# A hybrid attention and retention layer on one core: output jobs behind the next unit's query jobs, halves added in PSUM, a third job bank, x loaded transposed

## What is computed

```python
h = rms_norm(x, norm_gain)
proj = jnp.einsum('bsd,de->bse', h, w_in)
aq, ak, av, ag, rq, rk, rv, rg = jnp.split(proj, SPLIT_POINTS, axis=-1)
attn = window_attention(aq, ak, av, q_norm_gain, k_norm_gain, sink_logits)  # 16 heads, 4 kv heads, 64 wide, 2 chunks of 64
ret = retention(rq, rk, rv, ret_norm_gain)          # 8 heads, state carried over the chunks, group norm per head
mixed = jnp.concatenate([attn * jax.nn.silu(ag), ret * jax.nn.silu(rg)], axis=-1)
x = x + jnp.einsum('bse,ed->bsd', mixed, w_out)
```

## Time and profile before

| | |
|---|---|
| median of 3 runs | 1658.97 us (1658.12 to 1659.2) |
| the profiled execution's own time | 1657.89 us |
| its span, first to last instruction | 1656.1 us |
| busy PE / PEld | 96% / 83% |
| busy DVE / ACT / POOL | 70% / 41% / 27% |
| DMA | 320.49 MB, mean 194 GB/s |
| mean granted PE clock | 0.996 of 2.4 GHz |

### The profile page before, as it was taken

How to read it: one execution, slowest core, us unless ns; L and a number is a source line. 1 busy time by engine, 2 the same in 40 slices (tenths; PEclk the granted TensorE clock), 3 DMA queues, 4 the chain that set the end, 5 groups by cost and what they waited for, 6 DMA issues and landing times.

```text
span 1656.1 us, 24605 instructions
## 1 busy us (share of the span) xinstructions
PE 1598.1 (96%) x8320; PEld 1380.1 (83%) x8320; DVE 1166.8 (70%) x3045; ACT 673.7 (41%) x1985; POOL 450.8 (27%) x453
## 2 busy tenths in 40 slices
PE   5999999999999999999999999999999999999999
PEld 5778788787798888888888898888888888888887
DVE  6887768867868576684776757576686766757576
ACT  6543635535444242432444334241444414334241
POOL 5546446454412111121211212121121111212111
PEclk9999999999999999999999999999999999999999
DMA  9748567575774443546357353443547445353451
GB/s 309 280 147 309 200 215 267 185 249 206 245 293 145 176 180 125 200 156 216 125 196 286 135 203 139 170 191 118 213 171 267 181 173 189 129 203 133 171 197 51
DMA packets 151453, 320.49 MB, mean 194 GB/s; under 512 B 26272, under 2 KB 89888, under 8 KB 151328
## 3 DMA queue, kind: packets, MB, share of 16 engines
q1 hardware_dynamic: 151328, 318.91, 53.9%
HBM read 247.56 MB, written 71.30 MB: 193 GB/s over the span
## 4 chain that ended last, share of the span: by engine, by line
PE 51%; DVE 29%; ACT 13%; issue 5%; POOL 1%; DMA 0%; SPq 0%; DVEq 0%; ACTq 0%
PE jb L902 15%; PE jb L904 15%; PE jb L903 14%; ACT sx L417 6%; DVE sx L632 3%; DVE m L635 3%; DVE sx L630 2%; DVE qS L610 2%; DVE d L640 2%; DVE pTL L560 1%; DVE rawqn L603 1%; DVE rawqn L600 1%; ACT qS L400 1%; POOL rstd L303 1%; PE s L975 1%
## 5 line engine op out<-in xcount | busy, mean ns | idle before, releaser
L902 PE MATMUL jb<-wH,hTH 128*128 128x512 f32 (+1 forms) x1024 | 373.8, 365 | 0.0
L903 PE MATMUL jb<-wL,hTH 128*128 128x512 f32 (+1 forms) x1024 | 372.0, 363 | 0.0
L904 PE MATMUL jb<-wH,hTL 128*128 128x512 f32 (+1 forms) x1024 | 371.9, 363 | 0.0
L902 PE MATMUL jb<-wH,mxH 128*128 128x512 f32 x512 | 206.7, 404 | 10.8 <-DVE mxL L560 10.7
L904 PEld LDWEIGHTS jb<-wH,hTL 128*128 128x128 f32 x1024 | 192.8, 188 | 20.5
L902 PEld LDWEIGHTS jb<-wH,hTH 128*128 128x128 f32 x1024 | 193.4, 189 | 18.6
L903 PEld LDWEIGHTS jb<-wL,hTH 128*128 128x128 f32 x1024 | 193.0, 188 | 18.2
L902 PE MATMUL jb<-hTH,wH 128*128 128x512 f32 x512 | 203.4, 397 | 4.0 <-DVE gate L653 4.0
L903 PE MATMUL jb<-hTL,wH 128*128 128x512 f32 x512 | 201.2, 393 | 0.0
L904 PE MATMUL jb<-hTH,wL 128*128 128x512 f32 x512 | 201.1, 393 | 0.0
L904 PE MATMUL jb<-wH,mxL 128*128 128x512 f32 x512 | 200.6, 392 | 0.0
(11 more groups left out here) (148 smaller groups left out, 2973.6 us busy)
## 6 DMA issues: line engine op xcount, KB each, us to landing
wH<-scrH SPq DMA_DIRECT2D x144, 512.0 KB, 7.4
wL<-scrL SPq DMA_DIRECT2D x144, 512.0 KB, 8.1
scrH<-wH SPq DMA_DIRECT2D x48, 512.0 KB, 5.3
scrL<-wL SPq DMA_DIRECT2D x48, 512.0 KB, 6.0
wH<-scrH SPq DMA_DIRECT2D x48, 384.0 KB, 5.8
wL<-scrL SPq DMA_DIRECT2D x48, 384.0 KB, 6.5
stage<-w_in_dram SPq DMA_DIRECT2D x64, 256.0 KB, 4.5
acc<-x_dram SPq DMA_DIRECT2D x4, 2048.0 KB, 15.2
```

The lines of the kernel that those rows point to most:

```text
L902: pe.matmul(o, lh, rh_, start=i == 0, stop=False)
L903: pe.matmul(o, lh, rl_, start=False, stop=False)
L904: m = pe.matmul(o, ll, rh_, start=False, stop=i == last)
```

## The change

**Order.** A unit's phases are now Q of unit n, O of unit n-1, G of n, V of n. Unit 0 has no O among its phases; the last unit has Q, G, V, then both O phases. The steps A of tile 3, I of tiles 2 and 3 and all MT go into the next unit's Q and O phases; the steps of the attention spread over Q, O, G and V. Panels keep two buffers, now by their place in the new order.

**PSUM.** Jobs rotate over three banks. The scores and the retention's output take half the room: the H and L products go to the same columns, one after the other. The scores' four matmuls of 256 columns become eight of 128, and the retention output's eight (four of 256, four of 128) become twelve of 128. DVE's second instruction of `part1` and its addition in `gna` go away. S and I now share one bank `s2`, MT uses A's bank `ab`, and both add waits.

**x.** The host passes x also transposed and the weights laid out per panel (one DMA per chunk). PE turns only the row factors (`XB`, one transpose per tile), DVE multiplies (`h`), POOL makes the low half; the 8 transposes per tile go away. A few buffers shrink (`qS` to two tiles, `stage` to three chunks).

```diff
-STEPS = {
-    3: [("TQ", 0)], 4: [("TQ", 1)], 5: [("TQ", 2), ("S", 0)], 6: [("TQ", 3), ("S", 1)],
...
+def phases(n):
+
+    if n == 0:
+        return [("Q", 0), ("G", 0), ("V", 0)]
+    if n < LAST:
+        return [("Q", n), ("O", n - 1), ("G", n), ("V", n)]
+    return [("Q", n), ("G", n), ("V", n), ("O", n - 1), ("O", n)]
...
+STEPS_MID = {("Q", 0): [("A", -1, 3)], ("Q", 1): [("I", -1, 2), ("MT", -1, 0)], ("Q", 2): [("I", -1, 3)],
+             ("Q", 3): [("TQ", 0, 0), ("MT", -1, 1)],
+             ("O", 1): [("TQ", 0, 1)], ("O", 2): [("S", 0, 0), ("MT", -1, 2)], ("O", 3): [("TQ", 0, 2)],
...
+            return jb[JOB_AT[n, j] % 3]
...
                 for par in range(2):
                     win = slice((2 * t + par) * CHUNK, (2 * t + par + 2) * CHUNK)
                     for hp in range(2):
-                        m = pe.matmul(s_parts[:, par, hp], qS[:, t, 2 * hp + par], kHL[:, :, win], start=True, stop=True)
+                        for i in range(2):
+                            m = pe.matmul(s_parts[:, par, hp], qS[:, t % 2, 2 * hp + par], kHL[:, i, win],
+                                          start=i == 0, stop=i == 1)
...
-                    pe.matmul(o, rqH[:, a, cols], both(rHL[:, :, :]), start=True, stop=False)
-                    pe.matmul(o, aH[:, e], both(v), start=False, stop=False)
-                    pe.matmul(o[:, 0:P], rqL[:, a, cols], rHL[:, 0], start=False, stop=False)
-                    pe.matmul(o[:, 0:P], aL[:, e], v[:, 0], start=False, stop=True)
+                    pe.matmul(o, rqH[:, a, cols], rHL[:, 0], start=True, stop=False)
+                    pe.matmul(o, rqH[:, a, cols], rHL[:, 1], start=False, stop=False)
+                    pe.matmul(o, aH[:, e], v[:, 0], start=False, stop=False)
+                    pe.matmul(o, aH[:, e], v[:, 1], start=False, stop=False)
+                    pe.matmul(o, rqL[:, a, cols], rHL[:, 0], start=False, stop=False)
+                    pe.matmul(o, aL[:, e], v[:, 0], start=False, stop=True)
...
-                v.scalar_tensor_tensor(out=four(xs), in0=s_parts[:, :, :, 1], scalar=HD ** -0.5, in1=four(xs),
-                                       op0=ALU.mult, op1=ALU.add).then_inc(S["s_x"], 1)
...
-                v.tensor_tensor(oraw[:, :, :], oraw[:, :, :], ro_parts[:, :, 1], ALU.add).then_inc(S["s_oc"], 1)
...
+            def qkv_phase(n):
+
+                m = n - 1
+                rvg(m, 3); kw_am(m, 3); rl(m, 2)
...
+                qkv(n, 0); rupd(m, 2); rl(m, 3); kwl_al(m, 3); gnv(m, 1); gnb(m, 1); gna(m, 2)
+                qkv(n, 1); gnv(m, 2); mtl(m, 0); rupd(m, 3); carry_in(n); gnb(m, 2); gna(m, 3)
+                qkv(n, 2); gnv(m, 3); tql(n, 0); mtl(m, 1); gnb(m, 3)
...
-                for k in range(KT):
-                    m = pe.transpose(xbanks[t % 2][k // 4][:, (k % 4) * P:(k % 4 + 1) * P],
-                                     xbuf[t % 2][:, k * P:(k + 1) * P], ident[:, :])
-                m.then_inc(S["s_xT"], 1)
+                bank = ab[:, t * P:(t + 1) * P] if b else xbanks[t][:, 0:P]
+                pe.transpose(bank, xr[:, t:t + 1].broadcast_to([P, P]), ident[:, :]).then_inc(S["s_xb"], 1)
```

More of the change, by code:

```diff
@@ L446, in rvg @@
                     act.wait_ge(S["s_rvg"], nth(n, 4, t - 1))
[L447 removed]
+                act.activation(th[:, 0:256], bank[:, 256:512], ACT.Tanh, scale=0.5).then_inc(S["s_rvt"], 1)
             def obcopy(n, t):
@@ new lines, in _ @@
+            v.wait_ge(S["s_gains"], 16)
+            xms_(0, 0)
+            h(0, 0)
+            xl_first(0)
+            xms_(0, 1)
+            h(0, 1)
+            xl_first(1)
+            xms_(0, 2)
+            xms_(0, 3)
+            h(0, 2)
+            xl_first(2)
+            v.wait_ge(S["s_qkg"], 64)
+            carry_in(0)
+            qkv(0, 0)
+            h(0, 3)
+            xl_first(3)
+            qkv(0, 1)
+            qkv(0, 2); tql(0, 0)
+            qkv(0, 3); tql(0, 1); part1(0, 0)
@@ new lines, in _ @@
+            agg(0, 0); tql(0, 2); part2(0, 0); part1(0, 1)
+            agg(0, 1); tql(0, 3); part2(0, 1); rq_decay(0); ptl(0, 0); part1(0, 2)
+            mix(0, 0); ptl(0, 1); part2(0, 2); part1(0, 3); carry_out(0)
+            mix(0, 1); rl(0, 0); ptl(0, 2); kw_am(0, 0); kwl_al(0, 0); rvg(0, 0); part2(0, 3)
+            mix(0, 2); ptl(0, 3); kw_am(0, 1); rvg(0, 1); rupd(0, 0); rl(0, 1); kwl_al(0, 1); gna(0, 0)
+            mix(0, 3); rvg(0, 2); gnv(0, 0); kw_am(0, 2); kwl_al(0, 2); gnb(0, 0); rupd(0, 1); gna(0, 1)
@@ new lines, in _ @@
+            for n in range(1, LAST):
+                b, u = n // NU, n % NU
+                m = n - 1
+                qkv_phase(n)
+                qkv(n, 3); tql(n, 1); add(m, 0); mtl(m, 2); part1(n, 0); add(m, 1)
+                tql(n, 2); add(m, 2); part1(n, 1); add(m, 3); mtl(m, 3); part2(n, 0)
+                tql(n, 3); add(m, 4); ptl(n, 0); part2(n, 1); add(m, 5)
+                if b < NB - 1 and u == 2:
+                    for t in range(NT):
+                        xms_(b + 1, t)
+                late_phases(n)
@@ new lines, in _ @@
+            n, m = LAST, LAST - 1
+            qkv_phase(n)
+            qkv(n, 3); tql(n, 1); mtl(m, 2); part1(n, 0); agg(n, 0); mtl(m, 3); tql(n, 2); part2(n, 0); part1(n, 1)
+            agg(n, 1); tql(n, 3); part2(n, 1); part1(n, 2)
+            rq_decay(n); ptl(n, 0); part2(n, 2); part1(n, 3)
+            rl(n, 0); mix(n, 0); part2(n, 3)
+            kw_am(n, 0); kwl_al(n, 0); rvg(n, 0); ptl(n, 1)
+            kw_am(n, 1); rvg(n, 1); rupd(n, 0); rl(n, 1); kwl_al(n, 1); gna(n, 0)
+            kw_am(n, 2); rvg(n, 2); rupd(n, 1); rl(n, 2); kwl_al(n, 2); gnv(n, 0); gnb(n, 0); gna(n, 1)
@@ L1024 @@
+            XB(0, 0)
+            for n in range(UNITS):
+                iteration(n)
 _OUT_SHAPE = (1, SEQ, DM)
```

947 lines of the change are left out of this document (541 added, 406 removed), and 17 rows, old and new, of tables (STEPS_FIRST, STEPS_LAST, STEPS_MID).

## The result

The changed kernel takes 1789.3 us (median; 1787.6 to 1790.6) against 1658.9 (1658.1 to 1659.2) of the kernel before: ratio 1.0786, 95% interval 1.0768 to 1.0805. It is 130 us slower. The forecast was 1680, so the direction was right and the size six times too small.

The account below looks back on a forecast made before the run. PE, busy 96% of the span, was taken as the bound. Terms 52 - 9 - 14 - 5 - 3 = +21 on a span of 1656.1 gave 1677, predicted as 1680 us, range 1641 to 1700.

Parts of the forecast that it names:

- four gains: Savings set against the short matmuls' cost: turns -9, units 1 to 3 -14, start -5, waits in steady units -3.
- Short matmuls, +52: Steps S and I: 0.11 us per 128-column matmul, +0.41 and +0.40 in 64 tiles, +52 us (bounds -12 and +65).
- Units 1 to 3, -14: Early units with weight splits: half of their 27 us over steady units comes back, -14 us (bounds 0 and -27).
- Waits in steady units, -3: Old waits for mxL and gg go (20 us), new ones from DVE's order cost 17: net -3 us (bounds -17 and +20).
- Start, -5: Start and unit 0: G jobs some 3 us earlier, unit 0 wins 2 more, -5 us (bounds +3 and -12).
- Turns, -9: O phases of three units: 96 transposes costing about 13 us go, 4.4 in all stand in their place, -9 us.
- If the x tiles come late enough to stop DVE, this is lost: Condition on the turns' gain: late x tiles that stop DVE would lose the -9 us.
- A third bank takes away little: Job banks in PSUM: no wait for a job's bank among PE's three longest kinds, each under 7.1 us in the span.
- the third (DVE becomes the bound in Q and O): Rival: POOL's weight work slows DVE; steady waits +19, early units gain nothing (+14): 1713 us, chance 0.10.
- 4 more than before and not 8: DMA traffic: 8 MB more in 320, staying hidden, as a buffer's reload has a phase of 21 us or more.

Follow-up runs that it names:

- halves_only: The kernel before with halves of scores and retention outputs added in PSUM (8 and 12 matmuls), DVE's two adds per tile left out: 1686.1 us, ratio 1.0166.
- wh_early: The changed kernel with the weight-half copies of panels 1 and 2 written one place earlier on ACT and POOL: 1774.6 us.
- mixl_early: The changed kernel with POOL's low halves of the mix put between its weight subtractions from unit 1 on, not behind all eight: 1771.0 us.
- oraw3: The changed kernel with a third buffer for the raw retention outputs, so ocopy(m,3) waits for MT(m,0) and not MT(m,1): 1769.5 us.
- last_mid: The changed kernel with MT(-1,1) of the last unit at Q3 behind TQ0, in place of Q2: 1784.5 us.

## Why the forecast was right in direction and wrong in size

The forecast was a sum of +52 for short matmuls and -31 for four gains. In place of the -31 stand +80, if the short matmuls are taken at their price of 51. That the change would be slower was right for the forecast's one cost; the larger part of the 130 us is not in it.

- *Short matmuls, +52: the price is right.* A scores step takes 0.84 to 0.92, step I's matmuls start 0.11 apart, in the changed kernel and alone (halves_only). What the sum did not have: where PE waits anyway the price is not paid in full (28 of 52 came out in the old order). The Trainium skill (TensorE: Matmul & The Clock Gate, Back-to-back issue gap) has 81 ns for such pairs; all rows here show 110. By its figure the forecast would have been lower and the miss larger.
- *Units 1 to 3, -14: this step failed, found about +47.* I reasoned that steps with several jobs of room would lose their waits, and gave half of the 27 us back. The room exists for PE's steps but not for ACT, DVE and POOL, which each run a written order of their own: the weight work was written in behind instructions that wait for scores, and other work behind the weight work. Shown: the splits cost 26 us in the old and 74 in the new order; of these 48 more, wh_early returned 15 and mixl_early 18 by order alone, with the same splits; the other 15 stay open. I had seen both conditions ("POOL's low halves of G come late", "DVE is slowed where POOL works") and put a gain on them.
- *Waits in steady units, -3: nearly right,* 102.2 us for 101 to 102, thus 0.4 a unit over the short matmuls' price where the sum had 0.25 under it. But I listed the waits by DVE's order alone. The longest, TQ1's 0.9 a unit, came from `ocopy(m,3)` on ACT, which waits for MT(m,1). The prediction moved MT and did not ask who waits for it. oraw3 shows 1.4 us a unit.
- *The last unit: no term, found +19.* Its Q phase has an order of its own, and there lies most of it (14.7 us, see last_mid). last_mid gave 5 of it; the rest was not taken apart.
- *Start, -5: found +6.* The first job does start 12 us earlier (12.75 for the earlier trace rows's 24.96), but unit 0's four Q jobs with their steps take 37.1 us instead of 18.4. PE waits there 6.2 us for `kHL` at TQ1, 2.9 for `rawqn` at TQ0 and 3.0 for `hTL` (the other 3.7 for `hTL` stand ahead of the first job), and the clock's mean is 0.85. I put the start of the G jobs at 40, it came at 49.9, before at 43.3. Of the V jobs' 3.7 us more, 3.3 are a wait for `rkL`. The prediction named tiles that wait for their factors and DVE's multiplications, but worked out no size for them from rows; the wait for `kHL` was not in it. The earlier trace rows also leave out the longest kind of PE's waits before, 12.8 us in 2 for scaled rows of x, both ahead of the first job; this is part of what the earlier first job gains. No experiment took the start apart.
- *Turns, -9: found about -3.* The transposes went (three turns took 14.9 us of O phases before), but the Q phase behind a turn takes 24.5 us for 20.8 and the G phase ahead 0.9 more, about 4 a turn. In that Q phase step I of tile 3 waits 1.7 us for `kwL`, since DVE multiplies the last x tile first. In unit 8 (row below) the next job then runs in part at 1.2 GHz, and the window's clock is 0.93. In unit 12 the clock stays at 1.00, MT waits 1.5 us for `mxL` instead, and the phase takes the same 24.5 us: DVE's chain sets it, not the clock.

```profile
915.30:939.80 24.50, 22.83 (x136) 22.34 (x135) 18.74 (x58) 8.97 (x26) 9.54 (x9) 0.93 0.46 173
```

  "If the x tiles come late enough to stop DVE, this is lost" was the right condition, and it held.
- *"A third bank takes away little": wrong.* I read this off the waits of the old order, in which no wait for a bank shows. In the new order the out jobs stand beside the softmax work on DVE, and there the bank holds 50 us.
- *The clock was left out.* The earlier trace rows show 0.98 in unit 1. A wait of 5 us can cost more than 5, since PE runs at 1.2 GHz behind it. Over the span 107 us ran at the lower level, against 13; where PE had work in them and nothing else held it up, half of each is lost, so by this estimate up to 47 of the 130 us, and less where a wait would have followed anyway, as at the turns.

Of the rivals, the third (DVE becomes the bound in Q and O) had the right place and the right units, but it was priced at +14 there, on the thought that the early units could at worst gain nothing; its +19 in the steady units did not come.

The DMA moves 324.72 MB, 4 more than before and not 8, and no wait of PE is put down to a DMA, as forecast.

## What to carry to other kernels

When a step is moved, list everyone who waits for its result or its buffer on every engine, and for each queue what is written behind that waiter; the time it costs stands there and not at the moved step. A resource that nobody waits for in the old order may be what carries the new one. Stretches in which other engines have much to do (here units 1 to 3) are judged by their queues, and the bound engine's prices count only in part there; there give a change of order a range on both sides of zero.

## What the runs showed of the hardware

- DVE instructions were stretched beside POOL's subtractions of 512 columns (1.3 us each): a DVE multiplication of 64 columns took 1.28 us beside one and 0.22 without, one of 320 columns 1.47 and 0.49, and two multiplications into `mixr` 2.80 beside two others on POOL and 0.85 without. The added time is 1.0 to 1.1 us an instruction, a little under one subtraction on POOL. The Trainium skill (SBUF - State Buffer, "SBUF: two separate sides") says that a DVE instruction with two inputs in SBUF and a POOL instruction that reads SBUF exclude each other for a whole instruction; the rows agree. A cast on DVE (`veven<-vcar`, 1.30 for 0.21) and its multiplication by per-row factors (`oraw<-oraw,mv,grs`, 1.32 for 0.34) were stretched as well, and these have one tile as input. The same section names DVE's 2-port mode as a second case and gives for it an fp32 copy from SBUF to SBUF, which this cast is; no row here shows in which mode either of the two ran. Not every POOL instruction does this: beside `rstd<-ms,mhalf` (5 columns, 1.17 us from 257.75) two casts of 64 columns kept their 0.22 us.
- Each of PE's waits of about 5 us or more was followed by work at half the clock: matmuls of 512 columns 0.43 apart instead of 0.23, at a granted clock of 0.50 in the window from 272 to 276 us. The same followed both waits of 1.9 us (at 174 and 298 us). Of three waits of 1.7 us, one was followed by it (at 927 us) and two by full speed (at 430 and 1340 us), and the steady units' waits of 0.9 us were followed by full speed.
